# Opening of a hybrid DeltaNet and attention layer: order and buffers of its first loads changed

## Time and profile before

| | us |
|---|---|
| median of 3 runs | 1880.91 (1878.99 to 1881.01) |
| the profiled execution, its own time | 1878.7 |
| its span in the trace | 1876.5 |
| PE busy | 1800.9 (96%) |
| DVE busy | 909.9 (48%) |
| ACT busy | 661.4 (35%) |

### The profile page before, as it was taken

The page is one execution under the profiler, slowest core; times in us unless marked ns, Lnnn a source line. Parts: engine busy times, 40 slices in busy tenths (PEclk is TensorE's granted clock), DMA queues, the critical chain, the costliest instruction groups (busy, mean ns, idle before and its releaser), DMA issues.

```text
span 1876.5 us, 25273 instructions
## 1 busy us (share of the span) xinstructions
PE 1800.9 (96%) x10174; PEld 1441.6 (77%) x10174; DVE 909.9 (48%) x1595; ACT 661.4 (35%) x1211; POOL 278.1 (15%) x421
## 2 busy tenths in 40 slices
PE   5799999999999999999999999999998889999999
PEld 2367888888787888878888887877875566788887
DVE  1244443556524577545556554754455544453334
ACT  4323332223234555444343435422354333232211
POOL 0000000000003366377000003211000100210000
PEclk9899999999999999999999999999999999999999
DMA  8793112223224666645444337777432222652332
GB/s 303 245 326 124 57 57 57 63 73 90 70 60 153 197 181 182 203 149 146 136 126 131 115 94 226 231 213 211 140 113 87 87 87 73 257 191 96 118 124 101
DMA packets 198685, 267.12 MB, mean 142 GB/s; under 512 B 37073, under 2 KB 135626, under 8 KB 197162
## 3 DMA queue, kind: packets, MB, share of 16 engines
q1 hardware_dynamic: 175241, 192.74, 34.1%
q0 software_dynamic: 15552, 58.62, 9.4%
q10 hardware_dynamic: 7776, 14.16, 2.0%
HBM read 221.96 MB, written 43.52 MB: 141 GB/s over the span
## 4 chain that ended last, share of the span: by engine, by line
PE 85%; ACT 4%; DVE 4%; DMA 4%; issue 2%; POOL 0%; SPq 0%; ACTq 0%; DVEq 0%; POOLq 0%
PE psum L1610 23%; PE psum L1611 22%; PE psum L1612 22%; PE psum L1915 2%; PE psum L1758 2%; PE psum L1707 1%; PE psum L1709 1%; PE psum L1935 1%; PE psum L1902 1%; PE psum L1603 1%; PE psum L1715 1%; DVE w_lo L1091 1%; ACT w_hi L759 1%; PE psum L1711 1%; PE psum L1713 1%
## 5 line engine op out<-in xcount | busy, mean ns | idle before, releaser
L1091 DVE TENSOR_TENSOR w_lo<-w_raw,w_hi 128x1024 fp32r<-128x1024 f32 x232 | 290.7, 1253 | 625.9 <-ACT w_hi L759 625.6
L759 ACT ACTIVATE w_hi<-w_raw 128x1024 fp32r<-128x1024 f32 x232 | 245.6, 1058 | 864.5 <-PE psum L1612 774.6
L1610 PE MATMUL psum<-h_hi,w_hi 128*128 128x512 f32 x1152 | 470.8, 409 | 8.7 <-DVE w_lo L1091 6.4
L1611 PE MATMUL psum<-h_lo,w_hi 128*128 128x512 f32 x1152 | 452.6, 393 | 0.0
L1612 PE MATMUL psum<-h_hi,w_lo 128*128 128x512 f32 x1152 | 452.1, 392 | 0.0
L1610 PEld LDWEIGHTS psum<-h_hi,w_hi 128*128 128x128 f32 x1152 | 218.2, 189 | 68.2 <-issue 19.4
L1612 PEld LDWEIGHTS psum<-h_hi,w_lo 128*128 128x128 f32 x1152 | 217.5, 189 | 48.1
L1611 PEld LDWEIGHTS psum<-h_lo,w_hi 128*128 128x128 f32 x1152 | 218.5, 190 | 36.2
L1161 DVE SCALAR_TENSOR_TENSOR conv_acc<-conv_in,convw,conv_acc 128x772 f32<-128x772 f32 x96 | 98.2, 1023 | 3.4
L1610 PE MATMUL psum<-w_hi,m_hi 128*128 128x512 f32 x256 | 99.6, 389 | 0.0
L1611 PE MATMUL psum<-w_lo,m_hi 128*128 128x512 f32 x256 | 99.6, 389 | 0.0
(11 more groups left out here) (306 smaller groups left out, 2750.3 us busy)
## 6 DMA issues: line engine op xcount, KB each, us to landing
w_raw<-w_in_dram SPq DMA_DIRECT2D x168, 512.0 KB, 3.9
w_raw_mod<-w_mod_dram SPq DMA_DIRECT2D x64, 512.0 KB, 5.7
w_raw_modg<-w_mod_dram POOLq DMA_DIRECT2D x32, 512.0 KB, 4.5
w_raw<-w_out_dram SPq DMA_DIRECT2D x32, 512.0 KB, 3.6
gate_scratch<-gate_stage ACTq DMA_DIRECT2D x48, 256.0 KB, 4.4
w_raw<-w_proj_a_dram SPq DMA_DIRECT2D x16, 512.0 KB, 4.1
w_raw<-w_proj_b_dram SPq DMA_DIRECT2D x16, 512.0 KB, 3.4
gates<-gate_scratch POOLq DMA_DIRECT2D x32, 256.0 KB, 4.0
```

What stands on the lines that cost most here:

```text
L759: act.activation(part(whi[i % 2], p), part(place, p), ACT.Copy).then_inc(S("w_hi"), 1)
L1091: dve.tensor_tensor(part(wlo[i % 2], p), part(raw_of(n)[0], p), part(whi[i % 2], p).bitcast(f32), ALU.subtract).then_inc(S("w_lo"), 1)
L1610: pe.matmul(out_ap, lh, rh, start=first, stop=False, skip_group_check=shared)
L1611: pe.matmul(out_ap, lh, rl, start=False, stop=False, skip_group_check=shared)
```

## The change

Five things are changed together.

1. **Rows.** The five small loads into `rows` and the one into `conv_rows` are issued by ACT on its own queue. POOL waits for the five before it issues the first x tile. `conv_rows` has a semaphore of its own; PE transposes it at n = 3, into another bank, and DVE copies it at n = 5. The first mod piece no longer waits for it.
2. **x tiles.** Six buffers, one for each tile (four of them in space of h that is written later). The load of tile t waits until tile t-2 has landed, and no longer for PE. `X_AT = 1 + 2t`; PE's transposes and ACT's copies come at `X_AT + 4`.
3. **Mod ring.** Six buffers in place of four.
4. **Modulation vectors and h.** PE turns a group's sums to columns at `last + 2` (before: `last + 1`), DVE follows one n later, and `h_columns` stands at the same n as that. For the last group PE's step stands at `last`, and ACT's copy and DVE's steps at `last + 1`.
5. **Early k-tiles.** Each early piece stands four mod pieces sooner. Its split is at mod piece m-8 (with the load; before m-10). The piece at n = 69 (`BRIDGE`) is loaded after mod piece 58 (before 61), and its first k-tile runs behind the last mod piece, ahead of the last group's columns.

The semaphores of several memsets on POOL are also merged into one, in the same order of the same instructions.

```diff
-EARLY = {31: (0, 0), 39: (1, 0), 47: (0, 1), 55: (1, 1), 63: (0, 2)}
+EARLY = {27: (0, 0), 35: (1, 0), 43: (0, 1), 51: (1, 1), 59: (0, 2)}
...
-    BEFORE_LAST = {MOD_AT[m - 6 + 2 * kk]: (MOD_AT[m] + 1, kk) for m in EARLY for kk in range(3)}
+    BRIDGE = MOD_AT[63] + 1
+    BEFORE_LAST = {MOD_AT[63]: (BRIDGE, 0)} | {MOD_AT[m - 6 + 2 * kk]: (MOD_AT[m] + 1, kk) for m in EARLY for kk in range(3)}
...
-        SPLIT_AT[MOD_AT[m] + 1] = MOD_AT[m - 10]
-    SPLIT_AT[MOD_AT[63] + 2] = MOD_AT[59]
+        SPLIT_AT[MOD_AT[m] + 1] = MOD_AT[m - 8]
+    SPLIT_AT[BRIDGE] = MOD_AT[59]
...
-        LOADS += [MOD_AT[63] + 2] * (n == MOD_AT[61])
+        LOADS += [BRIDGE] * (n == MOD_AT[58])
...
-    X_AT = [1 + 3 * t for t in range(NT)]
-    H_AT = [max(g["last"] + 2, X_AT[-1] + 5) for g in MODS if g["scale"]]
-    H_AT[-1] -= 1
+    X_AT = [1 + 2 * t for t in range(NT)]
+    COLS_AT = [g["last"] + 2 for g in MODS[:-1]] + [MODS[-1]["last"]]
+    MODV_AT = [n + 1 for n in COLS_AT]
+    H_AT = [max(MODV_AT[gi], X_AT[-1] + 6) for gi, g in enumerate(MODS) if g["scale"]]
     H_PARTS_AT = [a + 1 for a in H_AT[:-1]] + [H_AT[-1]]
-    MODV_AT = [g["last"] + 2 for g in MODS[:-1]] + [MODS[-1]["last"] + 1]
...
-    raw_mod = [at(f"w_raw_mod{i}", [P, 1024], A_H + 32768 * (i // 2) + 24576 + 4096 * (i % 2)) for i in range(4)]
+    A_MODS = [A_H + 24576, A_H + 28672, A_H + 57344, A_H + 61440, A_C + 12288, A_C + 28672]
+    raw_mod = [at(f"w_raw_mod{i}", [P, 1024], a) for i, a in enumerate(A_MODS)]
+    RING_MOD = len(raw_mod)
...
-    xt = [at(f"x_rows{i}", [P, DM], A_G + 49152 + 8192 * i) for i in range(2)]
+    A_X = [A_G + 49152, A_G + 57344, A_H + 8192, A_H + 16384, A_H + 40960, A_H + 49152]
+    xt = [at(f"x_rows{t}", [P, DM], a) for t, a in enumerate(A_X)]
...
+            pool.wait_ge(S("rows_in"), 80)
             for t in range(NT):
                 if t >= 2:
-                    pool.wait_ge(S("xt_ready"), 4 * (t - 1))
+                    pool.wait_ge(S(f"x_in{t % 2}"), 16 * (t // 2))
...
-            act.wait_ge(S("cols"), 2)
+            for r0, n, src in ((0, 16, c[0, :]), (16, 16, c_ctx), (32, 16, norm_w[0, :]), (48, 48, b_mod[0, :]),
+                               (96, 1, a_norm_w[0, :])):
+                act.dma_start(rows[r0:r0 + n, :], src.rearrange("(t p) -> t p", p=P)).then_inc(S("rows_in"), 16)
+            act.dma_start(crows[:], conv_w[0].rearrange("t (c p) -> (t c) p", p=P)).then_inc(S("conv_rows_in"), 16)
+
+            act.wait_ge(S("cols"), 1)
...
-                piece(n, ks=(3,) if n in EARLY_AT else None)
+                piece(n, ks=(3,) if n in EARLY_AT else (1, 2, 3) if n == BRIDGE else None)
...
-                    if n == X_AT[t] + 3:
+                    if n == X_AT[t] + 4:
                         x_transposes(t)
...
-                for gi, g in enumerate(MODS):
-                    if n == g["last"] + 1:
+                if n == X_AT[1]:
+                    pe.wait_ge(S("conv_rows_in"), 16)
+                    pe.transpose(bank(5, 120), crows[:], ident[0:120, 0:120]).then_inc(S("rowsT"), 1)
+                for gi in range(len(MODS)):
+                    if n == COLS_AT[gi]:
                         mod_cols(mrow, 6 + gi % 2, "mod", gi + 1)
```

More of the change, by code:

```diff
@@ L535, in _ @@
             sp.dma_start(consts[:], consts_in).then_inc(S("const_in"), 16)
[L536 to L539, removed]
             for n in LOADS:
@@ L543, in _ @@
                     m = mods_made[n] - 1
-                    before = MOD_AT[m - 4] if m >= 4 else None
+                    before = MOD_AT[m - RING_MOD] if m >= RING_MOD else None
                 else:
@@ L579, in _ @@
             for i in range(2):
-                pool.memset(rawc[i][:], 0.0).then_inc(S("pads"), 1)
+                pool.memset(rawc[i][:], 0.0).then_inc(S("zeroed"), 1)
             pool.wait_ge(S("prep"), 1)
@@ L634, in _ @@
             decay_rhs(UNITS[0])
-            pool.memset(X64[:], 0.0).then_inc(S("inv_zero"), 1)
+            pool.memset(X64[:], 0.0).then_inc(S("zeroed"), 1)
             pool.wait_ge(S("kv_spill"), 16 * NT)
-            pool.memset(SS[:], 0.0).then_inc(S("states0"), 1)
+            pool.memset(SS[:], 0.0).then_inc(S("zeroed"), 1)
             for u in UNITS:
@@ L648, in _ @@
                 pool.wait_ge(S("decay_mm"), 2 * N_UNITS)
-                pool.memset(YY[d][:], 0.0).then_inc(S("inv_zero"), 1)
+                pool.memset(YY[d][:], 0.0).then_inc(S("zeroed"), 1)
             for b in (1, 2):
@@ L693, in _ @@
             for j in range(4):
-                pool.memset(gsum[j][:], 0.0).then_inc(S("gsum_zero"), 1)
+                pool.memset(gsum[j][:], 0.0).then_inc(S("zeroed"), 1)
             for j in range(4):
-                pool.wait_ge(S("gsum_zero"), j + 1)
+                pool.wait_ge(S("zeroed"), 6 + j + 1)
                 pool.dma_start(gsum[j][0:1, :], b_mod[0:1, 2 * DM + 512 * j:2 * DM + 512 * j + 512]).then_inc(S("gsum_bias"), 16)
@@ L764, in x_square @@
                     act.wait_ge(S("x_ssq"), t)
-                act.activation(junk[:], xt[t % 2][:], ACT.Square, accum_out=stat[:, t:t + 1]).then_inc(S("x_ssq"), 1)
+                act.activation(junk[:], xt[t][:], ACT.Square, accum_out=stat[:, t:t + 1]).then_inc(S("x_ssq"), 1)
             def x_std(t):
@@ L911, in _ @@
                 for t in range(NT):
+                    if n == X_AT[t] + 4:
+                        x_columns(t)
+                    if n == X_AT[t] + 1:
+                        x_std(t)
                     if n == X_AT[t]:
                         x_square(t)
[L914 to L917 removed]
                 for gi, g in enumerate(MODS):
@@ L1391, in _ @@
                         x_norm(t)
+                if n == X_AT[2]:
+                    dve.wait_ge(S("rowsT"), 2)
+                    dve.tensor_copy(convw[:], bank(5, 120)).then_inc(S("cols"), 1)
                 for gi in range(len(MODS)):
@@ L1563, in _ @@
             pe.wait_ge(S("const_in"), 16)
-            pe.wait_ge(S("rows_in"), 96)
+            pe.wait_ge(S("rows_in"), 80)
             pe.transpose(bank(0, 97), rows[:], ident[0:97, 0:97]).then_inc(S("rowsT"), 1)
-            pe.transpose(bank(1, 120), crows[:], ident[0:120, 0:120]).then_inc(S("rowsT"), 1)
             def x_transposes(t):
@@ L1575, in x_transposes @@
                         k = 4 * q4 + u
-                        ins = pe.transpose(bank4(n % 4)[:, u, :], xt[t % 2][:, k * P:(k + 1) * P], ident)
+                        ins = pe.transpose(bank4(n % 4)[:, u, :], xt[t][:, k * P:(k + 1) * P], ident)
                     ins.then_inc(S("xt_ready"), 1)
```

21 lines of the change are left out of this document (10 added, 11 removed).

## The result

| | before | after |
|---|---|---|
| median, us | 1879.95 (1876.03 to 1881.01, 4 runs) | 1855.34 (1852.45 to 1859.26, 4 runs) |
| ratio | | 0.9875 (0.9862 to 0.9889) |
| the profiled execution, us | 1878.7 | 1859.26 |
| its span, us | 1876.5 | 1857.1 |

24.6 us between the medians, against 19 forecast; 1855.3 lies 1.7 us under the stated range. The two profiled executions are 19.4 us apart. What the other 5 us are is the first question for the runs. (In all, 28 later executions of the kernel before took 1873.1 to 1881.8 us, with medians of 1877.3 to 1879.4 in three groups: the median of 1880.91 that the forecast was made from was a high one.)

A forecast was written before the change was run, and what follows sets the result against it. The opening's waits for small loads, x and first h were taken as the bound, then PE and DMA. Piece 69 ending at 144.5 (DMA-bound), not 163.5, saves 19.0: 1878.7 - 19.0 = 1859.7, plus 2.2, about 1862; range 1857 to 1872.

The forecast's parts named there:

- Rows: Start of the opening: five small loads issued from ACT take 3.4 us and land at 6.4 us.
- x: Opening: two tiles in flight at an equal share of 337 GB/s, 6.2 us a tile, the last landing at 43.6.
- Bytes: Opening: 18.9 MB before the first early k-tile, at 330 GB/s after 12 us, give 59.1; 60 taken.
- the other path of the sum: Opening: last x tile at 43.6, x complete at 50.4, `h_columns` at 52.7, first `h_lo` pair done at 58.2.
- PE-bound, 143.4: End of piece 69 if PE sets it: 60 + 79.9 + 3.2 + 0.3 = 143.4 us.
- The two new waits: PE waits for h at the third and fifth early pieces: 1.6 us each, 3.2, inside the DMA-bound time.
- The early k-tiles: Opening, k-tiles four mod pieces sooner: worth little alone, only spreading PE's work before the last weights land.
- From the profiled execution to the median: Last step of the sum: median 2.2 us above the profiled execution, so 1859.7 becomes 1861.9.
- Late x: Rival 1, opening: x at 7.8 us a tile, last at 53; gain 8 to 10, about 1872; chance 0.15.
- Late rows: Rival 2, opening: rows take 8.85 us from ACT too; gain 15, about 1866; chance 0.08.
- Faster than the bytes say: Rival 3, opening: full engines at 359 GB/s or more, no new waits; gain 26, about 1855; chance 0.10.
- Slower: Rival 4, opening: x stretched to 12.5 us a tile, end at 180; 16 us more, 1897; chance 0.03.

The follow-up runs named there:

- the interleaved kernel: Changed kernel with `h_lo` of each k-tile behind the next one's modulation, and splits of the first, third and fifth early piece one place sooner: 1850.53 us, ratio 0.9855.

## Why the prediction missed, by its steps

**The opening: its end within 2 us, but not by the bound that was named.** Forecast for the end of piece 69 was 144.5, by the weights; measured 142.7, by PE. In the profiled pair the gain was 19.4, forecast 19.0. That the stalls would go and the opening would be shorter by some 20 us is what the runs show; that it came so close is in part luck, as the steps show.

- *Rows* at 6.4: measured 8.1. The last of them was issued at 2.7 and took 5.4 us, not 3.4, inside the bounds of 3.0 and 8.85. The rule of the Trainium skill (DMA: Bandwidth & Descriptors, Rules for kernel authors) speaks of bandwidth; how long small loads take, it doesn't say. For these the two runs show that ACT's queue was no help and that what goes ahead or beside counts: from SP's queue ahead of the weights the rows are there at 5.0, from ACT's beside them at 8.1, and with x in the way too at 9.5.
- *x* at 6.2 us a tile: a mis-sized term. From 8.25 to 35.4 us are 27.2 us for six tiles, 4.5 each, under my own lower bound of 5.1. It was worked out from a stretch in which rows and constants also loaded. The equal share was wrong too: 6.3 MB in 27.2 us are 232 GB/s of about 400, more than half. The same page (Queues, rings and completion order) of the Trainium skill says that an engine takes turns between queues by packets. The trace agrees in direction only: x comes in rows of 8 KB and mod pieces in rows of 2 KB, and x got more than an equal share; no run here changed the size of a row. The term had little weight in the end, since x landed 8.6 us (35.4 to 43.98) before its last tile's turn came; with one tile in flight 2.7 us are lost.
- *Bytes* at 330 GB/s after 12 us: 372 from 12 to 50. I had taken the rate of a stretch in which PE set the pace (100 to 140) for the engines' limit. The first k-tile came at 58.2, not 60. That is the number of the other path of the sum (58.2 by `h_columns`), but by luck: the path had the last tile land at 43.6, it landed at 35.4, and the mod pieces that x had held up, the last of them until 37.9, put its turn off to 43.98. From there the path ran as forecast: `h_columns` at 52.77 for 52.7. At the end the weights were not the bound: the DMA share falls to 0.53 from 130 to 140 us.
- *PE-bound, 143.4*: this is what ran, 84.5 us from the first k-tile (58.19 to 142.68) for 83.4 forecast; the 3.4 us at half clock behind 58 us, worth 1.7, were not in the sum. (8.6/4 is 2.15 and not 2.17, which changes nothing.) The two new waits were forecast at 1.6 each and are 1.61 each. They were not covered by the weights, as I had it, but paid in full; in the interleaved kernel's trace they are gone.
- *The early k-tiles are worth little alone*: 0.6 us by the mark, 3.3 by the medians; not settled.

**From the profiled execution to the median: this step failed.** "The median of the runs shown is 2.2 above the profiled one: 1861.9" carries an offset of before over to after. It did not hold for before either: it came from three executions, and the 28 later ones have medians (1877.3 to 1879.4) on both sides of the profiled 1878.7. Nor was the clock of the long stretch full, as the prediction read it: the 1.00 of the window from 155 to 1876 us is rounded, and 10.2 us at half clock stood in it. Both profiled executions had as much behind the mark. The other three runs of after were 3.9 to 6.8 us shorter than its profiled one, and the second trace of after shows such an execution: 3.4 us at half clock, rest 4.6 shorter. In place of 2.2 above, after's median was 3.9 below its profiled execution. An execution's own spread of some 5 us belonged in the range and wasn't there. Fewer of such stretches than the trace that the sum was made against is a gain that no step of the change makes.

**What stays open.** The opening gives 20.4 us by two marks each; the two ratios give 23.5 (20.9 to 25.9) and 21.4 us (18.2 to 24.6). Whether the changed kernel also meets half clock less often behind the opening, or its executions fell so, the traces can't tell: its two show 10.2 and 3.4. The mean clocks of all executions point to less: 0.992 to 0.995, 0.993 in the mean, in eight of the changed kernel, against 0.986 to 0.993, 0.990 in the mean, in 28 of the kernel before. But they hold the opening too. Nor was each share of x buffers, tile spacing and later columns tried by itself; together with rows and early k-tiles they are the 11.7 us behind ring and split.

**The rivals.** Late x was the wrong way round. Late rows was half right (8.1), without its price. Faster than the bytes say named the time that was measured, about 1855, but did not happen as told: its gain of 26 had full engines and no new waits, the waits were there, and the opening gave 20.4. A kernel without the waits does reach it. Slower needed 9.8 us a tile; it was 4.5.

## What to carry to other kernels

Where loads feed a ring, count every stall of the consumer against the ring's depth in time: two more buffers of 512 KB were worth 8 us here, alone and in the changed kernel. But a part's worth depends on what stands beside it: beside the moved split alone the same buffers were worth 1.4 us, as both fill one gap. A wait that a plan hides behind a bound is only free if the bound is real; take a rate as a limit only from a stretch in which nothing else sets the pace. And make the range of a forecast from one profile at least as wide as the kernel's own executions differ, or read a mark inside the trace: between two traces of one kernel it moved by 0.5 and 0.8 us where the spans moved by 1.3 and 3.8. A mark is one execution's, though, and shares of 1 to 3 us need more than one.

## What the runs showed of the hardware

- TensorE's clock falls to its lower level for a few us in the middle of a kernel that is at 2.4 GHz otherwise, not in every execution and often at the same places (around 780, 1130 and 1202 us of the changed kernel), where PE had been partly idle: busy for 0.55 us from 776 to 780, 2.1 from 1124 to 1128, 2.8 from 1196 to 1200, of 4 each. The same idle time with the clock kept was seen too (2.4 us busy from 1124 to 1128 in the second trace). One such us costs about half a us where PE is the bound: rests of 1675.0 to 1676.2 with 3.4 us of it, 1677.1 to 1680.5 with 10.2 (and 1679.0 to 1679.9 with 13.6).
- The five small loads of `rows`, rows of 512 B, were there at 9.5, 8.1 or 5.0 us, and in the kernel before, together with `conv_rows`, at 12.5, by what shared the engines with them and what stood ahead in the queue; their own size was the same.
- With two x tiles and six mod pieces in flight the core loaded 394 to 425 GB/s from 12 to 30 us; the kernel before ran at 330 in the stretch (100 to 140 us) that I took for the limit. It was not without a price: one mod piece took 21.9 us from issue to landing meanwhile.
